# Waits between the scatters of a gate matrix in a mixer and expert-retrieval layer on one Trainium2 core

## What is computed

```python
q = einsum('td,dhq->thq', ht, w_query).reshape(T, 8, 2, 128)
scores = einsum('thpc,hpnc->thpn', q, sub_keys)          # 8 heads, 2 halves, 128 keys
s_top, i_top = top_k(scores, 16)
cand = s_top[..., 0, :, None] + s_top[..., 1, None, :]   # 256 pairs for each head
best, pos = top_k(cand, 16);  gates = softmax(best)      # 16 experts for each head
act = gelu(einsum('td,tkd->tk', h, expert_u[idx]))
out = einsum('tk,tkd->td', act * gates, expert_v[idx])   # 128 experts for each token
x = layer_norm(ALPHA * x + out)
```

## Time and profile before

| | |
|---|---|
| median of 3 runs (lowest to highest) | 1836.05 us (1828.1 to 1837.52) |
| span of the profiled execution | 1829.2 us |
| mean granted TensorE clock | 0.990 of full speed |
| busy: PE, DVE, ACT, POOL | 1783.8, 1257.4, 747.0, 1029.5 us |
| scatters (L521) | 384, busy 443.7 us, first at 632.3, last at 1276.8 |
| scoring tiles 14 to 55; pairs; tiles 120 to 127 | about 663 to 897; 897 to 1245; 1245 to 1294 us |
| value tiles | 1294.9 us to the end |

### The profile page before, as it was taken

How to read it: one execution, slowest core, us unless ns; L and a number is a source line. 1 busy time by engine, 2 the same in 40 slices (tenths; PEclk the granted TensorE clock), 3 DMA queues, 4 the chain that set the end, 5 groups by cost and what they waited for, 6 DMA issues and landing times.

```text
span 1829.2 us, 25762 instructions
## 1 busy us (share of the span) xinstructions
PE 1783.8 (98%) x9402; PEld 1513.4 (83%) x9402; DVE 1257.4 (69%) x2436; ACT 747.0 (41%) x1257; POOL 1029.5 (56%) x771
## 2 busy tenths in 40 slices
PE   9999999999999999999799999998999999999998
PEld 6777778887988878888699999996788878888886
DVE  6334261112588999798577787772599888888886
ACT  5734463222243323323356665652433333333331
POOL 6531424353253547787766776665588777777410
PEclk9999999999999999999899999999999999999999
DMA  5764633234132344445244444455999999999971
GB/s 195 253 216 136 199 113 103 82 106 182 58 116 72 128 134 145 138 135 161 92 141 157 157 163 148 145 167 162 325 383 373 391 389 385 363 364 372 368 275 69
DMA packets 189967, 368.69 MB, mean 202 GB/s; under 512 B 27905, under 2 KB 109953, under 8 KB 189714
## 3 DMA queue, kind: packets, MB, share of 16 engines
q1 hardware_dynamic: 101216, 209.74, 33.8%
q10 hardware_dynamic: 53810, 89.90, 13.8%
q0 software_dynamic: 34816, 67.41, 10.1%
HBM read 305.96 MB, written 61.01 MB: 201 GB/s over the span
## 4 chain that ended last, share of the span: by engine, by line
PE 89%; DVE 5%; ACT 2%; DMA 2%; another core or an unknown queue 1%; issue 1%; ACTq 0%; SPq 0%; DVEq 0%
PE bank L563 22%; PE bank L567 22%; PE bank L566 22%; PE bank L930 17%; DMA x<-in_x 1%; PE bank L846 1%; PE bank L699 1%; PE bank L726 1%; PE bank L712 0%; DVE cand L1713 0%; DVE cand L1738 0%; DVE weight L1739 0%; PE bank L770 0%; DMA gates<-gate_scratch 0%
## 5 line engine op out<-in xcount | busy, mean ns | idle before, releaser
L521 POOL DMA_INDIRECT gate_scratch<-scat_gate,scat_idx x384 | 443.7, 1155 | 197.4 <-issue 94.8
L471 POOL TENSOR_TENSOR w_lo<-stage,w_hi 128x1024 fp32r<-128x1024 f32 (+1 forms) x105 | 248.3, 2385 | 376.4 <-ACT w_hi L1013 340.5
L1013 ACT ACTIVATE w_hi<-stage 128x1024 fp32r<-128x1024 f32 (+1 forms) x284 | 292.4, 1043 | 225.0 <-PE bank L567 180.8
L563 PE MATMUL bank<-x_hi,w_lo 128*128 128x512 f32 (+1 forms) x864 | 338.2, 391 | 4.4 <-DVE w_lo L1617 2.9
L567 PE MATMUL bank<-x_hi,w_hi 128*128 128x512 f32 (+1 forms) x864 | 336.2, 389 | 0.5 <-issue 0.5
L566 PE MATMUL bank<-x_lo,w_hi 128*128 128x512 f32 (+1 forms) x864 | 335.9, 389 | 0.0
L567 PE MATMUL bank<-w_hi,wt_hi 128*128 128x512 f32 x768 | 299.7, 390 | 1.4 <-issue 1.4
L563 PE MATMUL bank<-w_hi,wt_lo 128*128 128x512 f32 x768 | 299.4, 390 | 1.6 <-DVE wt_lo L1869 1.4
L566 PE MATMUL bank<-w_lo,wt_hi 128*128 128x512 f32 x768 | 299.3, 390 | 0.5 <-issue 0.5
L1617 DVE TENSOR_TENSOR w_lo<-stage,w_hi 128x1024 fp32r<-128x1024 f32 x178 | 217.1, 1224 | 88.0 <-ACT w_hi L1013 48.9
L508 POOL DMA_INDIRECT gat<-in_expert_v,eidx x128 | 144.6, 1129 | 112.6 <-DVE bank L1601 74.6
(11 more groups left out here) (287 smaller groups left out, 3135.6 us busy)
## 6 DMA issues: line engine op xcount, KB each, us to landing
stage<-in_expert_uT SPq DMA_DIRECT2D x128, 512.0 KB
stage<-in_expert_v SPq DMA_DIRECT2D x128, 512.0 KB
stage<-in_mix_stream SPq DMA_DIRECT2D x84, 512.0 KB
gate_scratch<-zeros SPq DMA_DIRECT2D x32, 768.0 KB, 7.4
act<-activation_scratch ACTq DMA_DIRECT2D x32, 768.0 KB
gates<-gate_scratch ACTq DMA_DIRECT2D x32, 768.0 KB
activation_scratch<-act_out_a ACTq DMA_DIRECT2D x64, 256.0 KB
activation_scratch<-act_out_b ACTq DMA_DIRECT2D x64, 256.0 KB
```

What stands on the lines that cost most here:

```text
L471: nc.gpsimd.tensor_tensor(w_lo[:, slot, 0:width], stage[:, slot % STAGE, 0:width], w_hi[:, slot, 0:width], ALU.subtract).then_inc(split_do ...
L521: nc.gpsimd.indirect_dma_start(out=gate_cells, out_offset=bass.IndirectOffsetOnAxis(ap=scat_idx[:, b, k:k + 1], axis=0), in_=scat_gate[:, ...
L563: ins = mm(dst, l_lo, r_hi, start=first, stop=False)
L1013: act_f(w_hi[:, slot, 0:width], stage[:, slot % STAGE, 0:width], ACT.Copy).then_inc(hi_done, 1)
```

## The change

Three things are edited. (1) `BREATH` = 3: ahead of each cell whose number is a multiple of 3, except cell 0, POOL waits until every scatter issued so far in the block of the cell before it has landed; `in_block` counts them. (2) `PAIR_CELLS` goes from 208 to 216 and `LATE_CELLS` from 21 to 13, and the late cells are due over three tiles instead of five. (3) `FIRST_BEST_US` goes from 8.0 to 11.5, and the loop in `passed` no longer places splits beyond tile 55 (`PAIR_FIRST - 1`).

```diff
-FIRST_BEST_US = 8.0
+FIRST_BEST_US = 11.5
...
+BREATH = 3
-EARLY_CELLS, PAIR_CELLS, LATE_CELLS = 155, 208, 21
+EARLY_CELLS, PAIR_CELLS, LATE_CELLS = 155, 216, 13
...
-    return PAIR_END + (cell - EARLY_CELLS - PAIR_CELLS) * 5 // LATE_CELLS
+    return PAIR_END + (cell - EARLY_CELLS - PAIR_CELLS) * 3 // LATE_CELLS
...
+            in_block = [0] * DENSE
+
             def scatter(cell):
 
                 b, h, k = CELLS[cell]
+                if cell % BREATH == 0 and cell:
+                    before = CELLS[cell - 1][0]
+                    pool.wait_ge(scattered[before], 16 * in_block[before])
+                in_block[b] += 1
                 if k % HEAD_PICKS == 0:
                     pool.wait_ge(scat_ready, PH * b + h + 1)
                     if h >= 1:
...
-                while next_split[0] <= clock[0] / TILE_US + 3:
+                while next_split[0] <= min(clock[0] / TILE_US + 3, PAIR_FIRST - 1):
```

## The result

The changed kernel took a median of **2037.8 us** (2028.9 to 2046.4, 4 runs); the kernel before took 1832.4 us on the same chip (1828.1 to 1837.5, 4 runs). The ratio is 1.113, with a 95% interval of 1.108 to 1.118: slower, by 205 us. The profiled execution has a span of 2032.1 us and a mean granted TensorE clock of 0.939. The forecast was 2021 us in a range of 1949 to 2090.

The account below looks back on a forecast made before the run. TensorE was taken to bound the kernel before, and POOL's paused scatters, which delay the first gates, the kernel after: 1829.2 + 186 + 2 = 2017, plus half of 6.9 for the median, 2021 us; range 1949 to 2090.

Parts of the forecast that it names:

- The length of the train: POOL's 384 scatters with 127 pauses: three scatters and a pause take 7.16, 6.60, then 5.41 us, ending at 1467.
- a sign of being wrong: At POOL's pauses: the forecast is wrong if a pause's idle time comes out below 1.9 us.
- The rival with long landings: At POOL's pauses: landings of 3.59 us in the pairs and 2.73 in the quiet part, 2087 us; chance 0.10.
- From the train to the end: Start of the value stage: gates requested at 1469, landed 8.40 us later, PE starts 3.92 after; the rest as before.
- TensorE's wait: Ahead of the first value product: one wait of some 175 us, with POOL alone at work.
- the two named rows: PE's stalls of 10.53 and 5.86 us at the first and last pair, which may stay or go, hidden either way.
- The slack: POOL's waits for TensorE, 50 us, and 5.8 us before ScalarE asks for gates: what pauses could use up unseen.
- The other side: In the pairs: dense scatters hold up PE's releases and pauses cure it; 1808 us if a pause costs 0.8; chance 0.05.
- The counts 216 and 13: Due times of POOL's scatters: alone they bring the last scatter from 1276.8 to about 1262; cost and gain 0.
- VectorE's clock: At tile 14: its split moves ahead of the last head's long operations, the 2.92 us wait goes, 4.8 us gained.
- The estimate of 1959 us: At POOL's pauses: the forecast's sum if every pause cost the skill's 2.0 us.
- the rival with short landings: At POOL's pauses: landings of 1.91 us everywhere, train ends at 1398, 1949 us; chance 0.12.

Follow-up runs that it names:

- 24 pauses: Changed kernel with a wait for the newest scatter at one cell in sixteen instead of every third: 1843.6 us, ratio 1.026 to the kernel before.
- a limit of four under way: Changed kernel, every second scatter waiting for the pair of scatters before the last pair instead of the newest scatter: 1855.8 us, ratio 1.012 to the kernel before.
- the best kernel: Changed kernel, every fourth scatter waiting for the group of four before the last one instead of the newest scatter: 1788.7 us, ratio 0.995 to the kernel before.

## Why the prediction was right, and where its terms were off

**The step that decided** stood: each pause waits for the landing of the scatter ahead of it, 127 of them don't fit, the train becomes the bound, and everything up to TensorE's first value product hangs on it. The pauses alone and the rest alone (1.122 and 0.998) show that it is this edit and no other.

**The length of the train.** Forecast 1467, measured 1479 (1478.09 + 0.96). The steps of that sum, against the rows of after:
- Until 897: 102 cells from cell 12 on, 34 triples in 228 us, 6.7 us each instead of 7.16. Less 34 x 0.46 = 16 us. The pauses in it took 2.14 us on average, not 2.73.
- 897 to 1243: 142 / 3 = 47.3 triples in 346 us, 7.31 instead of 6.60. More by 34 us. Here the term was too small: with 157.08 / 142 = 1.106 us a scatter, 7.31 - 3.32 - 0.62 leaves 3.37 us for a pause.
- After 1243: 128 cells, 42.7 triples in 236 us, 5.53 each; the forecast makes about 240 of it. Once TensorE has stopped, a pause is 1.87 us (76.5 / 41 from 1262 to 1479 us), as forecast. But the shortest are 1.42, so "no landing is below 1.91" was a statement on the seven rows I had and not on the chip. 24 of the pauses are below the 1.9 us that I had named as a sign of being wrong; the mean of all is 2.53.

-16 + 34 - 4 gives 14, against the 12 measured. That the train came out so near is in part luck: two of its errors had opposite signs, which the total doesn't tell.

The seven landing waits that gave my mean come from both stretches. Six are in the earlier trace rows; the seventh, cell 192, stands among the pairs of the kernel before:

```profile
970.20 0.96 POOL L521 DMA_INDIRECT gate_scratch<-scat_gate,scat_idx  x1 [1.94 <-DMA gate_scratch<-scat_gate,scat_idx]
```

The three before 897 us have a mean of 2.14 us, which is what the pauses there took; the four among the pairs have 3.17, near the 3.37 there. One mean of 2.73 for both was the mistake. The rival with long landings had 7.46 us a triple from 897 to 1243, nearer to 7.31 than my 6.60, but 2.73 for a pause of the last stretch, which was far too long.

**From the train to the end.** The request came 11.3 us later than forecast (1480.3), TensorE started 10.0 us behind it instead of 12.3, and the value stage took 541.8 us where I had 534.3 + 2. That makes 14.5, and the span is 2032.1 instead of 2017. The 2 us for the restart of TensorE's clock can't be told apart in it: the granted clock was 0.54 in the first 5 us (1490 to 1495) and 1.00 in the next five. The 5.5 us in the value stage I had not foreseen. In this execution TensorE has 4.7 us of idle time there put down to "issue", nearly all of it between 1611 and 1621 us, and its clock dips; on the chip at 1796.5 the value stage behind the same train took 532.0 us (2024.9 - 1492.95), without such waits. What makes these waits wasn't tried.

**TensorE's wait** was 230.0 us instead of some 175. The 175 didn't follow from my own sum: the first value product would have been at 1469 + 12.3 = 1481.3, and TensorE's last product of scoring ended at 1293.5, which makes 188. Of the other 42 us 9 are in the later end of the train; 33 are that TensorE came to the end of scoring at 1260.3, since its stalls and the wait at tile 14 had gone. I had written that these may stay or go, hidden either way, and the time bears this out. But I had priced them by the two named rows at 16.4 us, and tile 14 at 4.8, when tile 125 was in truth 32 us late: 1281.53 before, 1249.41 after. The earlier trace rows show waits of 20.7 us; what makes up the rest I haven't taken apart.

**The slack** of 50 + 5.8 us was wrong in kind. It was slack against a TensorE that the scatters themselves had slowed. Where TensorE runs undisturbed, the last scatter without pauses starts at 1252.3, and the train is itself the last to be ready. This didn't touch the forecast, in which the train was built up from cell 12 without that slack, but it did make the expectation for 24 pauses miss by 40 us.

**The other side.** Its mechanism is real, which I had at 0.05 together with its price: dense scatters do hold TensorE up (1789 us with none, on a chip where the kernel before takes 1823), and with the pauses TensorE doesn't stall (1.7 us of waits against 22.1, both on the chip at 1838 us). What fell was the price, as stated: a pause of 0.8 us. With tile 125 at 1249.4 it would be less still: (1249.4 - 669.05) / 124 = 4.68 us a triple, less 3.33 for three scatters of 1.11 and 0.62 leaves 0.7. The shortest pause is 1.42, so the point isn't in reach of a wait for the newest scatter.

**The counts 216 and 13** were only measured together with the clock. Where the train without pauses is the last to be ready, as on the chip at 1796.5 us, they may have a share in what follows. **VectorE's clock**: the split moved ahead of the long operations (658.55), the wait at tile 14 went, and with the counts it is 4 us on the chip at 1796.5 us. That is near the 4.8 forecast, by which cell 12 starts earlier; it starts at 669.05 there, against 673.91 in the earlier trace rows.

**The skill's figure.** The Trainium skill, "DMA: Bandwidth & Descriptors", section "Anatomy of one DMA — SWDGE (gpsimd) path", gives about 2.0 us as fixed cost. The pauses in the quiet part are near it (1.87 on average), those beside other transfers are not (3.37 at 164 GB/s). But a pause only begins when POOL is done with its scatter: from the start of the scatter to the end of the pause it is 0.96 + 1.87 = 2.83 us even in the quiet part. The estimate of 1959 us came out 79 us short. Like 1949 and 2087, it lacks the 3.5 us that the forecast adds for the median of the runs.

**Two small slips.** For the rival with short landings I counted three of six rows; two are near 1.91 (cells 32 and 64), and the seventh row, cell 192, is the third. And of the 127 pauses one, ahead of cell 6, cost nothing (0.17 us idle): that scatter stands behind a split of POOL.

**Open.** Why dense scatters stop TensorE: the trace puts most of the idle time down to "issue" or a `kept` of ScalarE, and names no resource. It isn't shown whether the transfers do it or GpSimd's work in issuing them. A gap between the scatters helps; a limit of four under way doesn't, and a lower one was only tried together with a gap. One trait of the stretch in which TensorE nearly stops may bear on it: from 1230 to 1382 us the trace has no packet of the queues that load instructions, and the next one comes at 1383.6, 1 us after the next run of matmuls without idle time between them starts (1382.67); in the kernel before they start at most 28.3 us apart from 890 to 1285. But TensorE ran nine matmuls without idle time from 1255.27 on with no such packet near, so whether this is a cause or only follows from a TensorE that needs few new instructions isn't shown. Nor is it known why the same kernel stalls on the chips at 1823 and 1838 us, and in the result at 1832, while on the two at 1796 us no run shows a stall.

## What to carry to other kernels

A wait for the landing of the DMA just issued costs its whole latency on the queue that issues; if a limit is wanted, wait for one issued some groups ago, with a semaphore of its own. Before a wait is put into a long hidden train, build the train up from its instructions and compare its end with the consumer's; slack read off a profile may belong to a consumer that the train itself slows. A mean over rows from quiet and busy stretches hides two prices: take for each stretch the rows that stand in it. Here that would have given 2.14 and 3.17 us, where 2.14 and 3.37 were measured.

## What the runs showed of the hardware

- 128-element scatters from GpSimd back to back (one per 1.26 us, 14 GB/s in all) cut TensorE on one chip to a matmul per 2.8 us for over 100 us. At one scatter per 2.1 us the same kernel, in the same run, had 1.2 us of waits in the scoring before.
- The same kernel differs by 2.3% between chips (1796.5 and 1838.0 us), and the scatters have at least a large part in it: without them the chip where it takes 1823.2 us comes to 1788.8, about the 1788.7 us of the best kernel on the chip at 1796.5.
- The idle time ahead of a scatter that waits for the one before is 1.42 to 1.94 us when nothing else runs, and up to 6.7 us beside transfers at 142 to 164 GB/s.
